# Retention values multiplied token-major, and a fourth tile ahead of the last row of the dilated closing projection

## The chip, the cores and the metric

The kernel runs on one core of a Trainium2 chip. The metric is the device time of one execution in microseconds, as the median of three runs. Everything is computed in fp32: each large product of a weight matrix and activations is made as three matmuls on rounded halves (weight high part times activation high part, high times low, low times high).

## What is computed

Two stacks run over 512 tokens of width 1024. The first has two layers that mix three kinds of attention. The second has a layer of retention with a convolutional feed-forward behind it, then a layer of dilated attention with the same. The change is in the second stack. Cut to what matters:

```python
def retention_mixer(h, w_in, w_out, gn_gain, pos):
    proj = h @ w_in                      # q, k, v and gate; 4 heads, v is 512 wide per head
    ...
    y = retention_chunkwise(q, k, v, log_gamma)
    mu = jnp.mean(y, axis=-1, keepdims=True)
    var = jnp.mean(jnp.square(y - mu), axis=-1, keepdims=True)
    yn = ((y - mu) * lax.rsqrt(var + GN_EPS)).reshape(B, S, dv) * gn_gain
    return (jax.nn.silu(g) * yn) @ w_out

def dilated_mixer(h, w_q, w_o, k_sh, v_sh, pos):
    ...                                  # three groups of windows, 16 heads
    return o @ w_o                       # the closing projection
```

Since the output y is a linear combination of values, taking each value's own mean over its 512 entries away makes the mean of y zero. The kernel does that, before it multiplies with the decayed scores. The input h is a normalised x: the gain goes into the operands, and the factor 1/rms of a token is applied to the product.

## The kernel before

**Layout.** Activations lie channel-major: 128 channels on the partitions, 512 tokens along the free axis, eight tiles k = 0 to 7 (`KT`). The operand of a projection is the pair `HH` and `HL` (high and low part). One output tile of 128 channels is a PSUM bank of 128x512. It takes eight steps of `kt` (L689), and each step is three matmuls with a 128x128 block of weights as the stationary and 512 tokens as the moving operand (L696 to L698).

**Weights.** They come as one stream of blocks in the order in which PE uses them, eight blocks to a chunk, in a ring of three slots. SP loads a chunk, ACT rounds it to `w_hi` (L1196, one for each chunk, once PE is through with the chunk three back), POOL subtracts to get `w_lo` in two halves (L554, L556). The order of the stream is laid out on the host (L2420 to L2442); `beside` interleaves tiles that are multiplied together, k by k.

**Order.** Each engine has its own hand-written program for each stage; they meet by semaphores alone. PE counts steps in `kt_done`, DVE counts emptied banks in `evicted`.

**Retention (PE L952, ACT L1455, DVE L2132), for each of four heads.**
- Four value tiles, channel-major, in banks 0 to 3. DVE multiplies each with the row `RSTD` of 1/rms into `RVF2` (L2146). PE turns it with four 128x128 transposes into bank 6 (`turn`, L953, L961), and ACT copies that into the token-major `RVT` (`v_out`, L1278). In head 0 the first three tiles are multiplied side by side (`together`); the sum of squares, the spread of 1/rms over a bank and the first turn stand behind the fourth.
- Once all four tiles are turned, ACT takes the sum over each token's 512 values (L1481), and DVE adds the negated mean to `RVT` (`centre`, L2152). `centre` stands in DVE's program behind the rotation of both queries and keys (L2157 to L2169).
- Two query and two key tiles in banks 0 to 3, a gate tile in bank 0 and half of another in bank 1. Then the scores of four key blocks (L1004) in banks 4 and 5 by turns, each multiplied with the decay by DVE (L2206), the other half of the gate tile, the product of scores and values (L1018) in banks 6 and 7, and two more gate tiles in banks 2 and 3.
- The previous head's four outputs are finished on DVE between the next head's value tiles (`finish`, L2185 on: two multiplies, a rounding, a subtraction).

**Dilated attention.** Eight pairs of heads (`pair`). While a pair's attention runs, PE multiplies the projections of the next pair. In the last pair there are none, and PE does steps of the closing projection instead: rows k = 0 to 6 of its first three output tiles, 21 steps, in four groups (`out_steps`). Row k needs pair k's output `DO` rounded by ACT (`out_hi`, L1535) and its low part from DVE (`out_lo`, L2288). Rows 0 and 1 are made at the start of the last pair. Row 7 is the last pair's own output: DVE L2319, ACT L1375, DVE L2038. Behind it `linear` does the last row of the three tiles (L900 to L906), then five whole tiles.

```python
t.up("operand")
pe.wait_ge(sems["operand"], t.at("operand"))
for bank in range(3):
    self.kt(bank, hi, lo, KT - 1, False, True)
```

Of the kernel before, what the change touches and what calls it, by code (L numbers as in the profile page):

```python
# [125 lines left out]
for _n, _k in (("mix0", MIX_K), ("ple0", PLE_K), ("mix1", MIX_K), ("ple1", PLE_K), ("ret", RET_K + RETOUT_K),  # L126
# [30 lines left out]
    "decayed", "small", "y_copied", "v_mean", "centred", "ret_squared", "sq_added",  # L157
# [146 lines left out]
def two_stacks_kernel(nc, d, out):  # L304
# [3 lines left out]
    with ExitStack() as ctx:  # L308
# [90 lines left out]
        RVF2 = at("ret_vf", [P, SEQ], 44 * T1)  # L399
# [27 lines left out]
        INV = RC1  # L427

# [148 lines left out]
        def dilated(e):  # L577
            e.dilated()
            e.linear(3, KT, "dil", 1)
# [39 lines left out]
        RS0, RTURN = 4, 6  # L619
        ROTATION = 7  # L620
# [19 lines left out]
        def _(pe):  # L640
            t = Tally(pe)

            class Programs:
# [45 lines left out]
                def kt(self, bank, hi, lo, k, start, stop):  # L689

                    slot, w = self.n // SLOT % RING, slice(self.n % SLOT * P, (self.n % SLOT + 1) * P)
                    if self.n % SLOT == 0:
                        pe.wait_ge(sems["lo_half"], self.n // SLOT + 1)
                    elif self.n % SLOT == SLOT // 2:
                        pe.wait_ge(sems["lo_done"], self.n // SLOT + 1)
                    pe.matmul(banks[bank][:], WH[slot][:, w], hi[:, k, :], start=start, stop=False)  # L696
# [255 lines left out]
                def retention(self):  # L952
                    def turn(tile):  # L953

                        pe.wait_ge(sems["evicted"], tile + 1)
                        if t.k.get("v_token", 0):
                            pe.wait_ge(sems["v_token"], t.at("v_token"))
                        if t.k.get("ret_squared", 0):
                            pe.wait_ge(sems["ret_squared"], t.at("ret_squared"))
                        for b in range(QT):  # L960
                            ins = pe.transpose(banks[RTURN][:, b * P:(b + 1) * P], RVF2[:, b * P:(b + 1) * P], ID[:])  # L961
                        ins.then_inc(sems["v_turned"], t.one("v_turned"))
                        t.up("v_token")
# [6 lines left out]
                    for h in range(RET_HEADS):  # L970
                        v = self.tiles
                        if h == 0:
                            self.together([self.open(b) for b in range(3)], HH, HL, KT, KT)
                            self.open(3)
                            half(3, 0)
                            self.all_squares(OUTB, SQ2)
# [1504 lines left out]
```

## Time and profile before

| | |
|---|---|
| median of three runs | 3018.32 us (3017.38 to 3022.89) |
| profiled execution, its own time | 3016.4 us |
| its span in the trace | 3014.6 us |
| granted TensorE clock, mean | 0.99 of full speed |
| PE busy | 2953.8 us, 98% of the span |
| DVE, ACT, POOL busy | 1734.2, 1055.7, 1282.0 us |
| retention, heads (stretch of the trace) | 1263.8 to 1593.9 us |
| dilated attention, last pair | 2563.7 to 2592.1 us |

"Idle before" in brackets behind a row is the time that the engine stood still before it, and what ended that. Matmul ends are modelled, so the distance from start to start is the one to read. The span lies inside the execution's own time; 1.8 us lie around it.

### The profile page before, as it was taken

Reading aid. Unit: us, or ns where it says so; the run is one execution under the profiler, and the core shown is the slowest. Engines: PE = TensorE matmul, PEld = TensorE weight load, DVE = VectorE, ACT = ScalarE, POOL = GpSimd, SP = SyncE. Lnnn points to the kernel's source line nnn. Section 1 sums busy time; section 2 is a strip of 40 time slices with the busy share of each in tenths; the row PEclk is TensorE's granted clock in tenths of the full one; section 3 lists DMA queues with packets and bytes.
Section 4 is the critical chain, followed back from the end, with each engine's and each line's share of the span. In section 5 each row is a group of like instructions: output and inputs, shape, how many; then the busy total and the mean of one; then the engine's idle time right before and its main releaser. Section 6 shows DMA issues by size and latency. Waiting matters only on the chain.

```text
span 3014.6 us, 39189 instructions
## 1 busy us (share of the span) xinstructions
PE 2953.8 (98%) x15272; PEld 2357.2 (78%) x15272; DVE 1734.2 (58%) x3007; ACT 1055.7 (35%) x1875; POOL 1282.0 (43%) x926
## 2 busy tenths in 40 slices
PE   8999999999999999999999999998999999899998
PEld 6777778877777778877778788886888888688886
DVE  4765455475654555745553587615766666487722
ACT  4444342344443432533332322224333333432221
POOL 3333334453333345534444455544444434355543
PEclk9999999999999999999999999999999999999999
DMA  5222223232222223322222233332222222223332
GB/s 195 78 82 66 70 78 98 84 108 67 84 64 70 78 92 98 103 79 77 77 84 84 77 98 98 98 98 88 78 78 78 78 76 79 64 84 98 98 98 70
DMA packets 78332, 260.22 MB, mean 86 GB/s; under 512 B 10731, under 2 KB 13547, under 8 KB 78149
## 3 DMA queue, kind: packets, MB, share of 16 engines
q1 hardware_dynamic: 77572, 255.63, 27.3%
q8 instruction: 122, 2.00, 0.3%
q10 hardware_dynamic: 576, 2.10, 0.2%
q14 instruction: 62, 0.50, 0.1%
HBM read 255.53 MB, written 6.09 MB: 87 GB/s over the span
## 4 chain that ended last, share of the span: by engine, by line
PE 93%; DVE 4%; ACT 1%; DMA 1%; issue 1%; POOL 0%; SPq 0%; PEldq 0%; DVEq 0%; ACTq 0%; PEld 0%
PE bank L696 27%; PE bank L698 27%; PE bank L697 26%; PE bank L811 2%; PE bank L858 2%; PE bank L838 1%; PE bank L1018 1%; DVE x_res L1788 1%; PE bank L727 1%; PE bank L1054 1%; PE bank L817 1%; DMA bias_copies<-bias_vectors 1%; PE bank L1092 1%; PE bank L1075 1%; DMA w_raw<-in_w 0%
## 5 line engine op out<-in xcount | busy, mean ns | idle before, releaser
L554 POOL TENSOR_TENSOR w_lo<-w_raw,w_hi 128x512 fp32r<-128x512 f32 x458 | 611.3, 1335 | 1649.2 <-ACT w_hi L1196 1649.2
L696 PE MATMUL bank<-h_hi,w_hi 128*128 128x512 f32 x2656 | 1064.9, 401 | 17.9 <-DVE h_lo L1776 6.7
L698 PE MATMUL bank<-h_hi,w_lo 128*128 128x512 f32 x2656 | 1040.2, 392 | 0.0
L697 PE MATMUL bank<-h_lo,w_hi 128*128 128x512 f32 x2656 | 1038.7, 391 | 0.0
L1196 ACT CAST w_hi<-w_raw 128x1024 fp32r<-128x1024 f32 x458 | 480.0, 1050 | 1267.5 <-PE bank L698 1248.0
L556 POOL TENSOR_TENSOR w_lo<-w_raw,w_hi 128x512 fp32r<-128x512 f32 x458 | 667.7, 1458 | 35.9
L696 PEld LDWEIGHTS bank<-h_hi,w_hi 128*128 128x128 f32 x2656 | 501.9, 189 | 129.5 <-issue 22.8
L698 PEld LDWEIGHTS bank<-h_hi,w_lo 128*128 128x128 f32 x2656 | 501.0, 189 | 108.4
L697 PEld LDWEIGHTS bank<-h_lo,w_hi 128*128 128x128 f32 x2656 | 502.5, 189 | 98.3 <-issue 0.6
L2057 DVE TENSOR_SCALAR m<-bank,gains 128x512 f32<-128x512 f32 x48 | 36.1, 751 | 334.5 <-ACT ta L1392 200.3
L1327 ACT ACTIVATE probs<-probs,small_columns 128x128 f32<-128x128 f32 (+2 forms) x192 | 102.0, 531 | 167.2 <-DVE small_columns L1835 163.0
L698 PE MATMUL bank<-f_hi,w_lo 128*128 128x512 f32 x352 | 136.9, 389 | 0.0
L696 PE MATMUL bank<-f_hi,w_hi 128*128 128x512 f32 x352 | 136.9, 389 | 0.0
L697 PE MATMUL bank<-f_lo,w_hi 128*128 128x512 f32 x352 | 136.9, 389 | 0.0
L1830 DVE CUSTOM_DVE_ANT_0 probs<-bank,bias 128x256 f32<-128x256 f32 (+3 forms) x128 | 56.5, 441 | 92.1 <-PE bank L811 88.5
L696 PE MATMUL bank<-zo_hi,w_hi 128*128 128x512 f32 x192 | 77.3, 403 | 0.0
L1337 ACT COPY pt<-bank 128x256 f32<-128x256 f32 (+3 forms) x160 | 55.5, 387 | 62.1 <-PE bank L838 62.0
L696 PEld LDWEIGHTS bank<-f_hi,w_hi 128*128 128x128 f32 x352 | 66.1, 188 | 13.8
L697 PEld LDWEIGHTS bank<-f_lo,w_hi 128*128 128x128 f32 x352 | 66.1, 188 | 13.8
L698 PEld LDWEIGHTS bank<-f_hi,w_lo 128*128 128x128 f32 x352 | 66.1, 188 | 13.5
L698 PE MATMUL bank<-zo_hi,w_lo 128*128 128x512 f32 x192 | 75.0, 391 | 0.0
L697 PE MATMUL bank<-zo_lo,w_hi 128*128 128x512 f32 x192 | 74.8, 390 | 0.0
(288 smaller groups left out, 3950.6 us busy)
## 6 DMA issues: line engine op xcount, KB each, us to landing
w_raw<-in_w SPq DMA_DIRECT2D x458, 512.0 KB, 3.5
bias_copies<-bias_vectors SPq DMA_DIRECT2D x1, 2560.0 KB
x_res<-in_x_t ACTq DMA_DIRECT2D x4, 512.0 KB, 8.2
bias<-bias_copies SPq DMA_DIRECT2D x8, 256.0 KB, 3.3
bias<-bias_copies SPq DMA_DIRECT2D x16, 128.0 KB, 2.4
out_x<-x_res SPq DMA_DIRECT2D x8, 256.0 KB, 2.0
bias_copies<-bias_vectors SPq DMA_DIRECT2D x1, 1280.0 KB
ple_raw<-in_p_t SPq DMA_DIRECT2D x2, 512.0 KB, 3.6
```

Source lines behind the costliest of these rows:

```text
L554: pool.tensor_tensor(WL[slot][:, 0:half], RAW[slot][:, 0:half], WH[slot][:, 0:half].bitcast(F32), ALU.subtract).then_inc(sems["lo_half"], 1)
L556: pool.tensor_tensor(WL[slot][:, half:], RAW[slot][:, half:], WH[slot][:, half:].bitcast(F32), ALU.subtract).then_inc(sems["lo_done"], 1)
L696: pe.matmul(banks[bank][:], WH[slot][:, w], hi[:, k, :], start=start, stop=False)
L697: pe.matmul(banks[bank][:], WH[slot][:, w], lo[:, k, :], start=False, stop=False)
L698: pe.matmul(banks[bank][:], WL[slot][:, w], hi[:, k, :], start=False, stop=stop).then_inc(sems["kt_done"], 1)
L811: ins = pe.matmul(banks[S0 + m][:, 0:blocks * P], AQ[r, q], keys[r, kk], start=True, stop=(kind != "mla"))
L858: ins = pe.matmul(banks[OUTB][r, i * P:(i + 1) * P], v, p[:, b * P:(b + 1) * P], start=(b == 0), stop=(b == blocks - 1))
L1196: act.copy(WH[slot][:], RAW[slot][:]).then_inc(sems["hi_done"], t.one("hi_done"))
L1327: act.activation(s, s, ACT.Exp, bias=sm(NM + u), accum_out=sm(DEN + u)).then_inc(sems["exped"], t.one("exped"))
L1337: act.copy(p[:, 0:w], banks[TURN + m][:, 0:w]).then_inc(sems["pt_copied"], t.one("pt_copied"))
L1830: dve.tensor_tensor_reduce(SS[i % 2][m][:, 0:w], banks[S0 + m][:, 0:w], bias, 1.0, LOWEST, ALU.add, ALU.max, sm(MX + u)).then_inc(sems["dv ...
L2057: dve.tensor_scalar(m[:, tile, :], bank[:], gain(f"{g}{l}", tile), None, ALU.mult).then_inc(sems[step], t.one(step))
```

## The change

1. **Retention values.** The four value tiles of a head become four blocks of 128 tokens with all 512 value channels each. The activations are the stationary operand and 512 columns of weights the moving one. The four blocks take turns at every k, in banks 6, 7, 2 and 3, with three matmuls each. The number of matmuls and their sizes stay: 4 x 8 x 3 of 128x512. `RVF2`, `turn` and its transposes go, and so do the ACT copies of them.
2. **Scaling and centring.** 1/rms is now a factor for each partition; the four columns are kept in `small_columns` (one small DVE copy, once). ACT reads each bank once, scales it and sums it (`accum_out`); DVE negates and divides the sum, and writes the scaled and centred block from the bank to `RVT`. `centre` stands ahead of both rotations.
3. **Order in retention.** In head 0 the sum of squares stands behind k = 4 and the spread behind k = 7, in bank 4. In the other heads the spread stands behind k = 1 and all four `finish` ahead of `centre`.
4. **Closing projection of the dilated layer.** PE does k = 0 to 6 of a fourth tile ahead of the wait for row 7, and then row 7 of all four. Four whole tiles follow.
5. **First operands.** Rows 0 and 1 are made by ACT and DVE at the end of the last but one pair, once its third query tile is through. In the last pair ACT waits for each row by itself.

The weights' order on the host follows. The core of the diff:

```diff
@@ PE
+                        self.rot = 3
+                        fourth = self.rotate()
+                        for k in range(KT - 1):
+                            self.kt(fourth, hi, lo, k, k == 0, False)
                         t.up("operand")
                         pe.wait_ge(sems["operand"], t.at("operand"))
-                        for bank in range(3):
+                        for bank in (0, 1, 2, fourth):
                             self.kt(bank, hi, lo, KT - 1, False, True)
-                        self.rot = 3
...
-                    def turn(tile):
...
+                    def values(k):
+
+                        slot, w = self.n // SLOT % RING, slice(self.n % SLOT * P, (self.n % SLOT + 4) * P)
+                        self.weights_in()
                         for b in range(QT):
...
+                            if k == 0:
+                                self.open(RVALUES[b])
+                            q, out = slice(b * P, (b + 1) * P), banks[RVALUES[b]]
+                            pe.matmul(out[:], HH[:, k, q], WH[slot][:, w], start=(k == 0), stop=False)
+                            pe.matmul(out[:], HL[:, k, q], WH[slot][:, w], start=False, stop=False)
+                            pe.matmul(out[:], HH[:, k, q], WL[slot][:, w], start=False, stop=(k == KT - 1)).then_inc(sems["kt_done"], 1)
+                        self.n += 4
...
+                        for k in range(KT):
+                            if h == 0:
+                                pe.wait_ge(sems["operand"], t.at("operand", k + 1 - KT))
+                            values(k)
+                            if (h, k) == (0, 4):
+                                self.all_squares(RS0, SQ2)
+                            elif (h, k) == (0, KT - 1):
+                                self.spread(RS0)
+                            elif h and k == 1:
+                                self.spread(RS0)
+                        for j in range(4):
                             self.whole(self.open(j))
...
-                        t.up("centred", QT)
-                        pe.wait_ge(sems["centred"], t.at("centred"))
-                        pe.wait_ge(sems["v_token"], t.at("v_token"))
+                        pe.wait_ge(sems["evicted"], v + QT)
@@ ACT
+                        self.past(4, KT)
+                        if h == 0:
+                            t.up("columns_kept")
+                            act.wait_ge(sems["columns_kept"], t.at("columns_kept"))
+                        for b in range(QT):
+                            act.wait_ge(sems["kt_done"], self.n - QT + b + 1)
+                            act.activation(RVT[:, b, :], banks[RVALUES[b]][:], ACT.Copy, scale=sm(XINV + b),
+                                           accum_out=sm(MX + b)).then_inc(sems["v_mean"], t.one("v_mean"))
+                        self.past(4, KT)
...
                         for k in range(2 * i, min(2 * i + 2, KT - 1)):
+                            act.wait_ge(sems["o_used"], self.o + k + 1)
                             act.copy(H2H[:, k, :], DO[:, k, :]).then_inc(sems["operand_hi"], t.one("operand_hi"))
...
+                        if before_last:
+                            act.wait_ge(sems["kt_done"], n + 7 * KT)
+                            out_hi(0)
@@ DVE
+                    row(RS0)
+                    dve.tensor_copy(sm(XINV, QT), sm(INV, QT)).then_inc(sems["columns_kept"], t.one("columns_kept"))
...
                     def centre():
...
+                        self.n += 4 * KT
+                        for b in range(QT):
                             t.up("v_mean")
                             dve.wait_ge(sems["v_mean"], t.at("v_mean"))
-                            dve.tensor_scalar(RVT[:, kt, :], RVT[:, kt, :], sm(MX + kt), None, ALU.add).then_inc(sems["centred"], t.one("centred"))
+                            dve.tensor_scalar(sm(NM + b), sm(MX + b), -1.0 / RET_V, None, ALU.mult).then_inc(sems["dve_step"], t.one("dve_step"))
+                            dve.wait_ge(sems["dve_step"], t.at("dve_step"))
+                            self.tiles += 1
+                            dve.tensor_scalar(RVT[:, b, :], banks[RVALUES[b]][:], sm(XINV + b), sm(NM + b), ALU.mult, ALU.add).then_inc(sems["evicted"], 1)
...
+                        centre()
                         rotary(RQ, 0)
                         rotary(RK, 2)
-                        centre()
...
                             u2(0)
+                            if z == KT - 2:
+                                out_lo(0)
                         else:
-                            out_lo(0)
```

## Rows read from the trace of the kernel before

**Rows 1.** The page: span, busy time of the engines, chain that ended last.

```profile
span 3014.6 us, 39189 instructions
...
PE 2953.8 (98%) x15272; PEld 2357.2 (78%) x15272; DVE 1734.2 (58%) x3007; ACT 1055.7 (35%) x1875; POOL 1282.0 (43%) x926
...
PE 93%; DVE 4%; ACT 1%; DMA 1%; issue 1%; POOL 0%; SPq 0%; PEldq 0%; DVEq 0%; ACTq 0%; PEld 0%
```

**Rows 2.** Waits of PE, whole span: who waited for whom, total us, times, longest.

```profile
PE bank L696 <- DVE h_lo L2038: 3.2, 1, 3.2
PE bank L696 <- DVE h_lo L2288: 1.9, 1, 1.9
```

**Rows 3.** Timeline of PE, head 0: start us, duration, instruction, shapes, count.

```profile
1270.06 0.39 PE L696 MATMUL bank<-h_hi,w_hi 128*128 128x512 f32 x1
...
1275.50 0.39 PE L696 MATMUL bank<-h_hi,w_hi 128*128 128x512 f32 x1
...
1294.74 0.60 PE L961 MATMUL bank<-ident,ret_vf 128*128 128x128 f32 x4
...
1300.67 0.60 PE L961 MATMUL bank<-ident,ret_vf 128*128 128x128 f32 x4
```

**Rows 4.** Windows, heads 0 and 1: length, busy by engine, clock, DMA share, GB/s.

```profile
1263.80:1347.75 83.95, 82.21 (x364) 65.11 (x365) 36.98 (x47) 29.06 (x43) 33.29 (x24) 1.00 0.29 95
1347.75:1429.80 82.05, 81.83 (x365) 65.02 (x364) 44.18 (x53) 26.87 (x39) 33.92 (x24) 1.00 0.26 77
```

**Rows 5.** Timeline, head 0: last sum of squares, first turn.

```profile
1271.98 0.69 DVE L2071 TENSOR_TENSOR sq<-sq 128x512 f32<-128x512 f32 x1
...
1288.76 0.66 PE L961 MATMUL bank<-ident,ret_vf 128*128 128x128 f32 x4 [1.51 <-DVE ret_vf L2146]
```

**Rows 6.** Timeline of DVE, head 1: first and last instruction of one `finish`.

```profile
1354.95 0.74 DVE L2185 SCALAR_TENSOR_TENSOR tc<-ret_y,gains,bank 128x512 f32<-128x512 f32 x1
...
1358.83 0.69 DVE L1621 TENSOR_TENSOR ret_lo<-tc,ret_hi 128x512 fp32r<-128x512 f32 x1
```

**Rows 7.** Timeline, head 0: end of the rotation, centring, scores.

```profile
1314.22 1.67 DVE L2161 TENSOR_TENSOR tc<-tb,ret_sin 128x512 f32<-128x512 f32 x1
...
1319.81 3.59 DVE L2152 TENSOR_SCALAR ret_vt<-ret_vt,small_columns 128x512 f32<-128x512 f32 x4
...
1320.66 3.17 PE L1004 MATMUL bank<-ret_q,ret_k 128*128 128x512 f32 x8
1324.06 1.57 PE L1004 MATMUL bank<-ret_q,ret_k 128*128 128x256 f32 x8 [0.22 <-DVE ret_p L2206]
```

**Rows 8.** Timeline, start of the last dilated pair: ACT, DVE and PE.

```profile
2563.28 0.19 ACT L1516 ACTIVATION_READ_ACCUMULATOR dil_p<-dil_p,small_columns 128x1 f32 x1
2566.67 2.18 ACT L1535 CAST h_hi<-dil_out 128x512 fp32r<-128x512 f32 x4
...
2564.79 0.32 DVE L2281 TENSOR_SCALAR dil_p<-dil_p,small_columns 128x192 f32<-128x192 f32 x1
2565.03 1.08 DVE L2319 TENSOR_SCALAR dil_out<-bank 128x512 f32<-128x512 f32 x1
2567.32 1.29 DVE L2288 TENSOR_TENSOR h_lo<-dil_out,h_hi 128x512 fp32r<-128x512 f32 x2 [1.21 <-ACT h_hi L1535]
...
2568.07 0.50 PE L696 MATMUL bank<-h_hi,w_hi 128*128 128x512 f32 x1 [1.88 <-DVE h_lo L2288]
```

**Rows 9.** Timeline and windows, end of that pair: PE, POOL, granted clock (third last).

```profile
2590.15 1.92 PE L1099 MATMUL bank<-dil_pc,dil_vt 128*64 128x128 f32 x32
2595.30 0.79 PE L696 MATMUL bank<-h_hi,w_hi 128*128 128x512 f32 x1 [3.23 <-DVE h_lo L2038]
...
2590.85 1.27 POOL L556 TENSOR_TENSOR w_lo<-w_raw,w_hi 128x512 fp32r<-128x512 f32 x1
...
2568.00:2572.00 4.00, 3.93 (x17) 3.28 (x18) 3.82 (x14) 3.45 (x11) 0.00 (x0) 1.00 0.00 0
2595.30:2598.00 2.70, 2.70 (x6) 2.14 (x7) 0.48 (x1) 0.00 (x0) 0.00 (x0) 0.50 0.62 194
```

More of the change, by code:

```diff
@@ L687, in rotate, with weights_in @@
                     return self.open((self.rot - 1) % of)
-                def kt(self, bank, hi, lo, k, start, stop):
-                    slot, w = self.n // SLOT % RING, slice(self.n % SLOT * P, (self.n % SLOT + 1) * P)
+                def weights_in(self):
                     if self.n % SLOT == 0:
@@ L695, in kt @@
                         pe.wait_ge(sems["lo_done"], self.n // SLOT + 1)
+                def kt(self, bank, hi, lo, k, start, stop):
+                    slot, w = self.n // SLOT % RING, slice(self.n % SLOT * P, (self.n % SLOT + 1) * P)
+                    self.weights_in()
                     pe.matmul(banks[bank][:], WH[slot][:, w], hi[:, k, :], start=start, stop=False)
@@ L971, in retention @@
                         v = self.tiles
[L972 to L976, printed above, removed]
-                            half(3, KT // 2)
-                            self.spread(OUTB)
-                            turn(v)
-                        else:
-                            for j in range(4):
-                                self.whole(self.open(j))
-                                if j == 0:
-                                    self.spread(RS0)
-                                else:
-                                    turn(v + j - 1)
-                        self.whole(self.open(0))
-                        turn(v + (1 if h == 0 else 3))
-                        for j in range(1, 4):
+                        for k in range(KT):
[9 more added lines that the diff above has]
+                        for j in range(4):
                             self.whole(self.open(j))
-                            if h == 0 and j < 3:
-                                turn(v + j + 1)
                         self.whole(self.open(0))
@@ L2047, in linear @@
                         if tile == 0:
[L2048 removed]
+                            self.n += KT - 1 + 4 if name == "dil" else first * nk
                         elif tile >= first:
@@ L2191, in retention @@
                     for h in range(RET_HEADS):
-                        for j in range(4):
-                            value(h, j)
-                            if h:
+                        if h:
+                            for j in range(4):
                                 finish(h - 1, j)
@@ L2421, in lay_out @@
     for h in range(RET_HEADS):
-        v = plain(ri, 2 * D + RET_V * h, 4)
-        stream += beside(*v[0:3]) + v[3:] if h == 0 else v
+        stream += beside(*plain(ri, 2 * D + RET_V * h, 4))
         stream += plain(ri, 256 * h, 2) + plain(ri, D + 256 * h, 2) + plain(ri, 4 * D + RET_V * h, 4)
@@ L2441, in lay_out @@
     wo = plain(a["att_w_o_2"][0])
-    stream += beside(*wo[0:3]) + wo[3:]
+    stream += beside(*(x[:, :KT - 1] for x in wo[0:3])) + [wo[3][:, :KT - 1]] + beside(*(x[:, KT - 1:] for x in wo[0:4])) + wo[4:]
     stream += up_and_down(1)
```

67 lines of the change are left out of this document (11 added, 56 removed).

## The prediction

> **What bounds the kernel now.** I read the page first. PE is busy 98% of the span, and the chain that ended last lies on it for 93% [rows 1]. So only three things can shorten this kernel: work of PE that goes away, stops of PE that go away, and slow clock. The waits of PE come next. Among them are two single stops at the lines that the change touches in the dilated layer, 3.2 and 1.9 us [rows 2]. Then I went through PE's timeline by stage for its distances from start to start. Two plain matmuls of 128x512 that are 24 apart start 5.44 us apart, 0.227 us each, and that in the stretch of head 0 where three banks take turns [rows 3]. Two turns of value tiles with the same 24 matmuls between them are 5.93 us apart [rows 3]. Whole heads take 83.95 us for the first and 82.05 for the others (heads 2 and 3 repeat head 1 within 0.1), at granted clock 1.00 [rows 4]. DVE and ACT have room (58% and 35% [rows 1]), so what moves between them costs nothing unless PE waits for it.
>
> **Part 1, the values on PE.** The 96 big matmuls of a head stay 96 of the same shape. I take the same 0.227 us for them, since stationary and moving operand only change places and both sides are 128 and 512 wide as before. The four transposes of a turn go: 5.93 - 5.44 = 0.49 us a turn, with what they cost the matmul behind them. Four tiles in four heads make 16 turns: **7.8 us**. The first turn of head 0 also waited 1.51 us for DVE, which had to spread 1/rms and scale a tile first [rows 5]. Behind the new spread stands a query tile that waits for nothing: **1.5 us**.
>
> **Part 2, scaling and centring.** In each head the third block of scores waited 0.22 us for DVE, whose first multiply with the decay stood behind 3.59 us of centring [rows 7]. With the centring ahead of the rotations DVE is free when the first scores arrive. Four heads make 0.9 us; between nothing (the multiply itself becomes the limit) and 0.9 I take **0.9**, as the whole 3.59 us moves away.
> The new centring is hidden, and this is its cover. ACT reads each block in about 0.55 us (a quarter of 2.18) and 0.19 for the sum; DVE needs at most 0.90 us (a quarter of 3.59) and 0.32 for a small step, 4.9 us for four blocks [rows 7, 8]. In heads 1 to 3 it queues behind four `finish`, each 4.57 us (1354.95 to 1359.52) [rows 6], 18.3 together. They start when 1/rms is spread, some 6.4 us into the values (8 steps of three matmuls, and about 1 us, an estimate, for column sums and spread), and end 24.7 us in; the values end near 22.8. So the centring ends near 29.6. The first reader is the third tile behind the values, which reopens bank 2 at 22.8 + 10.9 = 33.7. The cover is 4.1 us; it would be gone at 5.6 us a `finish`. If it is, each further microsecond is a microsecond of PE in three heads.
> Head 0: the last sum of squares ends at 1272.67 [rows 5], and PE wants it after five k of twelve matmuls, 13.6 us behind 1263.8, at 1277.4. No wait. Gate tiles and value blocks at the seam of two heads: block 3 needs the bank of the last gate tile, but nine matmuls (2.0 us) stand between, against one multiply of DVE, 0.69 in the rows nearest to it [rows 5]. Nothing.
>
> **Part 3, the fourth tile ahead of row 7.** Here PE stood 3.23 us, while DVE, ACT and DVE again made row 7 [rows 9]. Now it has 21 matmuls to do, 4.8 us that were due later anyhow. The stop goes: **3.2 us**. Behind the stop the clock was granted at 0.50, the 1.2 GHz level, and six matmuls took 2.70 us in place of 1.36. Behind the stop of 1.88 us the clock stayed at 1.00 [rows 9]. Without the long stop I expect no drop: **1.3 us**, between nothing and 1.3. The weights for it: the steps from the fourth on need the chunk whose first half is ready at 2590.85 [rows 9], while PE is there only at 2592.1 + 2.0. That four tiles and not three end at once gives ACT and DVE one more to empty, beside a next tile of 5.44 us that needs none of their banks. Nothing.
>
> **Part 4, rows 0 and 1 a pair sooner.** PE stood until 2568.07 for the low part of row 0 [rows 8]. ACT is free from 2563.47 and then rounds two rows in 1.1 us, by 2564.6; DVE ends the probabilities at 2565.11 and then makes row 0 by 2565.8. PE was there at 2568.07 - 1.88 = 2566.19. What is late next: DVE's output of pair 6 moves from 2565.03 to 2566.4, and its next scores start near 2567.5 in place of 2568.5, sooner, as the two subtractions no longer stand behind a wait for ACT. PE has 18 matmuls (4.1 us) ahead of the first thing that rests on them. I take **1.8 us**, between 1.0 (the lead of DVE's scores) and 1.9. In ACT's queue the added waits are for things long past (the third query tile, outputs 0 and 1), so nothing is held behind them.
>
> **Sum.** 7.8 + 1.5 + 0.9 + 3.2 + 1.3 + 1.8 = 16.5 us, against the profiled execution's own 3016.4 (span 3014.6 and 1.8 around it): 2999.9. The median of the runs lies 1.9 above that execution, so the forecast for the median is 3018.3 - 16.5 = **3001.8 us**.
>
> **Rivals.**
> *The token-major values lose the clock (slower).* Place: the value stretch, 96 matmuls a head that move to another bank after every three. If that brings small stops and the clock falls to 1.2 GHz, each costs 2.70/6 - 0.227 = 0.22 us more. All 384 cost 86 us, 3087 in all; it cancels the gain from 74 of them, a fifth. Against it: three banks already take turns in head 0, and there the distance is 0.227 us at clock 1.00 [rows 3, 4]. Chance 0.02.
> The Trainium skill (TensorE: Matmul & The Clock Gate, A second HAM failure mode: psum-queue depth-cycling) tells of just such a kernel, in which cycling through PSUM banks made PE idle briefly and its clock swing. By that rule this rival would come true; the rows of head 0 speak against it, since they cycle and stay fast.
>
> *The rotation comes late.* Keys were rotated by 1319.81, 0.85 us ahead of the scores at 1320.66 [rows 7]. Of the six multiplies behind the last key tile two took 1.67 us in place of 0.69. If the order of POOL's work beside them shifts and one more is slow, PE waits 0.1 us a head; if all four others are, 3.9 - 0.85 = 3.1, or 12 us in four heads: 3002 to 3014. Against it: POOL follows the stream of weights, which keeps its place against the key tiles. Chance 0.06.
> The Trainium skill (SBUF — State Buffer, Who interferes with whom) says that a DVE operation with two inputs in SBUF and a GpSimd operation that reads SBUF block one another for a whole instruction. The trace agrees: the 1.67 us row has two SBUF inputs.
>
> *The dilated part pays half.* The clock falls all the same behind the small products, or another wait takes the place of the two removed (the copied probabilities for the next products, say). The clock alone gives 3003; if half of the two stops stays too, 3005.5; if none of part 3 and 4 arrives, 3008.1. This is also the case of a change that doesn't do what it says. Against it: after rows 0 to 6 nothing in the fourth tile depends on the last pair. Chance 0.12.
>
> **How the numbers follow.** The forecast has chance 0.80. 3001.8 is its time. The range goes down to 2998.0 (a median 1 us low, as the lowest run of before, and two or three more us where other stops, such as other half-clock stretches, fall better) and up to 3009.0, which takes in the whole third rival and half of the second. A measurement of this kernel can tell about 0.2%, 6 us: faster than 3012.3 holds for the forecast, the dilated rival and most of the rotation's, 0.93; within it 0.05; slower 0.02.
>
> **What would show it.** Head 1 by the window from its first value matmul to the next head's: 82.05 - 2.0 - 0.2 = 79.9 us, head 0 near 80.3. No transposes at `turn`, matmuls in the values 0.227 apart, clock 1.00. The third block of scores without a wait. The stops of 3.2 and 1.9 us gone from PE's waits, and the row with clock 0.50 behind the first gone too. Wrong would be: distances over 0.227 in the values, a wait on `ret_k` or on the centring, a wait on `w_lo` in the fourth tile, or a new stop of PE in the last pair.

## The result, and the profile after

The median went from 3019.4 us to **2998.0 us** (2994.6 to 3000.4). Each kernel ran four times; the three runs given in front for before are among its four. The ratio is 0.9935, with a 95% interval from 0.9923 to 0.9947, so some 19.6 us or 0.65% went. The forecast was 3001.8 us and a clear gain. The measured median lies 3.8 us below it, at the low end of its range (2998.0) to within the rounding of the runs. The new median of before is 1.1 us higher than the one that the forecast started from, which makes the miss in the gain larger, not smaller: the medians lie 21.4 us apart and the ratio gives 19.6, where the sum said 16.5.

The page of the kernel after: span, busy time, and the chain that ended last.

```profile
span 2996.6 us, 38998 instructions
...
PE 2944.0 (98%) x15208; PEld 2350.6 (78%) x15208; DVE 1722.4 (57%) x3008; ACT 1046.8 (35%) x1859; POOL 1280.2 (43%) x926
...
PE 94%; DVE 3%; DMA 1%; ACT 1%; issue 1%; POOL 0%; SPq 0%; DVEq 0%; ACTq 0%
```

Against [rows 1] the span is 18.0 us shorter, and PE was busy 9.8 us less. PE issued 64 matmuls fewer, which are the sixteen turns of four transposes. So about half of the gain is work and slow clock that PE no longer has, and about half is time in which it stood. PE is still the bound.

The waits of PE after, the longest first (total us, times, longest):

```profile
PE bank L666 <- DMA table<-in_rel_bias: 10.2, 1, 10.2
PE bank L702 <- DVE h_lo L1761: 6.6, 2, 3.3
PE bank L742 <- DVE small_columns L1634: 5.6, 5, 1.4
```

Both rows of [rows 2] are gone, and none of these lies in a stage that was changed. (L702 to L704 are the three matmuls that were L696 to L698.)

**Retention.** Windows over heads 0 and 1 of the kernel after, and twelve us from the end of the last dilated pair over the last row (columns as in [rows 4]):

```profile
1266.23:1346.10 79.87, 79.87 (x349) 63.51 (x350) 34.47 (x48) 27.10 (x39) 33.12 (x24) 1.00 0.30 100
1346.10:1425.86 79.76, 79.76 (x350) 63.43 (x349) 41.07 (x53) 24.72 (x35) 33.45 (x24) 1.00 0.25 80
...
2577.00:2583.00 6.00, 6.00 (x50) 5.06 (x46) 2.98 (x3) 1.68 (x2) 5.01 (x5) 1.00 0.38 111
2583.00:2589.00 6.00, 6.00 (x28) 4.95 (x28) 0.87 (x2) 2.03 (x3) 3.05 (x4) 1.00 0.48 155
```

Head 0 lost 4.1 us and head 1 lost 2.3 [rows 4]; heads 2 and 3 take 79.76 and 79.74. The clock is 1.00 throughout, and PE's busy time is the whole window: no stop is left in a head. The value matmuls, which now change bank after every three, start 0.23 us apart, as before:

```profile
1347.23 0.40 PE L971 MATMUL bank<-w_hi,h_lo 128*128 128x512 f32 x1
1347.46 0.40 PE L972 MATMUL bank<-w_lo,h_hi 128*128 128x512 f32 x1
1347.70 0.40 PE L970 MATMUL bank<-w_hi,h_hi 128*128 128x512 f32 x1
1347.93 0.39 PE L971 MATMUL bank<-w_hi,h_lo 128*128 128x512 f32 x1
...
1369.05 0.39 PE L972 MATMUL bank<-w_lo,h_hi 128*128 128x512 f32 x1
```

From the second to the last of the 96 it is 21.82 us. That is 94 steps of 0.227 us and 0.47 us for the spread of 1/rms between them.

Scores of head 0, timeline of PE and DVE after; the rows of before are in [rows 7]:

```profile
1319.45 4.53 PE L1005 MATMUL bank<-ret_q,ret_k 128*128 128x512 f32 x16
1323.74 0.48 PE L702 MATMUL bank<-h_hi,w_hi 128*128 128x512 f32 x1
...
1326.57 2.75 PE L1017 MATMUL bank<-ret_p,ret_vt 128*128 128x512 f32 x9
...
1317.86 0.69 DVE L2148 TENSOR_TENSOR ret_k<-ret_k,tc 128x512 f32<-128x512 f32 x1
...
1321.43 0.69 DVE L2184 TENSOR_TENSOR ret_p<-bank,ret_decay 128x512 f32<-128x512 f32 x1 [2.88 <-PE bank L1005]
```

All sixteen matmuls of scores run in one go. DVE has been idle for 2.88 us when the first block arrives; before, it was in the middle of centring. The rotation of the keys ends at 1318.55, 0.90 us ahead of the scores (0.85 before). From the first score to the first matmul of the gate tile it is 4.29 us, against 4.73 in before (1320.66 to 1325.39). The wait that went had read 0.22 us, and 0.44 us went.

The new scaling and centring, head 1, on DVE and ACT: first and last instruction of the four `finish`, then the first block.

```profile
1353.12 0.75 DVE L2164 SCALAR_TENSOR_TENSOR tc<-ret_y,gains,bank 128x512 f32<-128x512 f32 x1 [3.47 <-PE bank L742]
...
1368.52 0.69 DVE L1606 TENSOR_TENSOR ret_lo<-tc,ret_hi 128x512 fp32r<-128x512 f32 x1
...
1370.48 0.68 ACT L1465 ACTIVATE ret_vt<-bank,small_columns 128x512 f32<-128x512 f32 x1
1371.06 0.19 ACT L1465 ACTIVATION_READ_ACCUMULATOR ret_vt<-bank,small_columns 128x1 f32 x1
...
1371.37 0.15 DVE L2128 TENSOR_SCALAR small_columns<-small_columns 128x1 f32<-128x1 f32 x1 [2.15 <-ACT ret_vt L1465]
1371.56 0.81 DVE L2131 TENSOR_SCALAR ret_vt<-bank,small_columns 128x512 f32<-128x512 f32 x1
```

Four `finish` take 16.1 us (18.3 were forecast). They end 2.15 us ahead of the first block, and so set nothing. The last block is written at 1375.09, 29.0 us into the head (forecast 29.6), and bank 2 is opened again 11 us behind the values, at 1380.15. By the forecast's reckoning that is 5.1 us of cover, where 4.1 were forecast. The block in bank 2 is the third of the four and is written by 1374.18, so the true cover is 6.0 us.

**The dilated part.** The start of the last pair (ACT, DVE), and the end of that pair (PE, DVE), after:

```profile
2552.04 1.12 ACT L1519 CAST h_hi<-dil_out 128x512 fp32r<-128x512 f32 x2
2553.70 1.28 DVE L2266 TENSOR_TENSOR h_lo<-dil_out,h_hi 128x512 fp32r<-128x512 f32 x2
2554.91 1.05 DVE L2298 TENSOR_SCALAR dil_out<-bank 128x512 f32<-128x512 f32 x1
...
2576.72 1.92 PE L1098 MATMUL bank<-dil_pc,dil_vt 128*64 128x128 f32 x32
2578.57 0.50 PE L702 MATMUL bank<-h_hi,w_hi 128*128 128x512 f32 x1
...
2580.49 1.38 DVE L2023 TENSOR_TENSOR h_lo<-dil_out,h_hi 128x512 fp32r<-128x512 f32 x1 [0.69 <-ACT h_hi L1374]
```

Row 0's low part starts 3.2 us behind the last products of pair 6 (2550.53), and PE's first step of the closing projection, at 2554.61, carries no wait; in before it carried 1.88 us [rows 8]. At the end of the pair PE goes from the products to the fourth tile without a stop. Row 7 is ready at 2581.87, while PE has work ahead until 2583.5. Behind it the clock stays at 1.00 (fourth window above), where before showed 0.50 [rows 9].

**Where the 18.0 us of the two traces lie.** I cut both traces at the same instructions:

| stretch | before | after | less |
|---|---|---|---|
| four heads | 330.13 | 319.13 | 11.0 |
| products of pair 6 to products of pair 7 | 28.29 | 26.19 | 2.1 |
| products of pair 7 to the sums behind the projection | 35.87 | 31.27 | 4.6 |
| all the rest, which no edit touches | 2620.3 | 2620.0 | 0.3 |

The last line hides larger differences that cancel: after loses 2.4 us ahead of the first retention head and gains 2.8 between the heads and pair 6. Half of that gain is a stretch of slow clock at the start of the feed-forward, which comes and goes in this form (granted clock of before, then of after at nearly the same instructions; it ends later in before, and the stretch around it, 1684.91 to 1718.65 there and 1676.36 to 1708.74 in after, is 1.4 us longer):

```profile
1691.30:1696.00 4.70, 4.66 (x11) 3.72 (x12) 4.18 (x7) 2.48 (x4) 0.00 (x0) 0.50 0.00 0
```

```profile
1682.30:1687.00 4.70, 4.68 (x13) 3.71 (x14) 4.18 (x7) 2.49 (x4) 0.00 (x0) 0.58 0.02 3
```

Over all profiles of this study, kernels with the same code there took 965.2 to 967.9 us from the end of the heads to the products of pair 6, and 1263.8 to 1269.7 us up to the first head. The total of a single profile is therefore good to some 6 us only. The stage distances repeat to 0.1 us wherever their code is the same (heads 319.1 in seven traces, pair 26.2 in ten, tail 31.27 in eight), and they are what I compare below. Most of the ratios below have intervals that overlap that of the changed kernel.

### The profile page after: what moved, and what is told of

It is laid out like the page before. It is cut to its first block, busy times and chain, and to the rows that moved or that the text cites. A ratio compares the mean times of both kernels' runs of the same rounds, so it can differ in the third digit from the quotient of the medians.

```text
span 2996.6 us, 38998 instructions
## 1 busy us (share of the span) xinstructions
PE 2944.0 (98%) x15208; PEld 2350.6 (78%) x15208; DVE 1722.4 (57%) x3008; ACT 1046.8 (35%) x1859; POOL 1280.2 (43%) x926
## 4 chain that ended last, share of the span: by engine, by line
PE 94%; DVE 3%; DMA 1%; ACT 1%; issue 1%; POOL 0%; SPq 0%; DVEq 0%; ACTq 0%
PE bank L702 26%; PE bank L704 26%; PE bank L703 26%; PE bank L817 2%; PE bank L864 2%; PE bank L844 1%; PE bank L1017 1%; PE bank L970 1%; PE bank L972 1%; PE bank L971 1%; DVE x_res L1773 1%; PE bank L1053 1%; PE bank L733 1%; DMA bias_copies<-bias_vectors 1%; PE bank L1005 1%; PE bank L823 1%
## 5 line engine op out<-in xcount | busy, mean ns | idle before, releaser
L702 PE MATMUL bank<-h_hi,w_hi 128*128 128x512 f32 x2528 | 1012.8, 401 | 11.7 <-DVE h_lo L1761 6.6
L704 PE MATMUL bank<-h_hi,w_lo 128*128 128x512 f32 x2528 | 990.0, 392 | 0.0
L703 PE MATMUL bank<-h_lo,w_hi 128*128 128x512 f32 x2528 | 989.3, 391 | 0.0
L702 PEld LDWEIGHTS bank<-h_hi,w_hi 128*128 128x128 f32 x2528 | 477.8, 189 | 118.0 <-issue 22.3
L704 PEld LDWEIGHTS bank<-h_hi,w_lo 128*128 128x128 f32 x2528 | 477.3, 189 | 103.2
L703 PEld LDWEIGHTS bank<-h_lo,w_hi 128*128 128x128 f32 x2528 | 478.2, 189 | 93.7 <-issue 0.6
L704 PE MATMUL bank<-f_hi,w_lo 128*128 128x512 f32 x352 | 137.0, 389 | 0.0
L702 PE MATMUL bank<-f_hi,w_hi 128*128 128x512 f32 x352 | 136.9, 389 | 0.0
L702 PE MATMUL bank<-zo_hi,w_hi 128*128 128x512 f32 x192 | 77.3, 403 | 0.0
L702 PEld LDWEIGHTS bank<-f_hi,w_hi 128*128 128x128 f32 x352 | 66.1, 188 | 13.8
L704 PEld LDWEIGHTS bank<-f_hi,w_lo 128*128 128x128 f32 x352 | 66.1, 188 | 13.7
L704 PE MATMUL bank<-zo_hi,w_lo 128*128 128x512 f32 x192 | 75.1, 391 | 0.0
```

Of the source, the lines that this page charges most:

```text
L703: pe.matmul(banks[bank][:], WH[slot][:, w], lo[:, k, :], start=False, stop=False)
L704: pe.matmul(banks[bank][:], WL[slot][:, w], hi[:, k, :], start=False, stop=stop).then_inc(sems["kt_done"], 1)
```

## Experiments

In the expectations, Theory A is the account by terms of the prediction, with the sizes that the trace after gave; the rival of each run stands in its own expectation. "Heads" is the time from the first value matmul of head 0 to the sums behind head 3, "pair" the distance from the products of pair 6 to those of pair 7, and "tail" that from there to the sums behind the projection. Before has 330.1, 28.3 and 35.9 us, after 319.1, 26.2 and 31.3.

### The retention part alone, the dilated part alone

The first run takes points 1 to 3 of the change and leaves points 4 and 5 as they were; the second takes points 4 and 5 alone. The edits are the hunks of the diff.

> The kernel before with the retention part of the change alone. Theory A (the gains are local: transposes, one wait, centring off the path): heads of 79.9, 79.8, 79.8, 79.7 us as in the changed kernel, 11.0 us less than before in the four; the last dilated pair as before (stops of 1.9 and 3.2 us, clock 0.50 behind the second). Time 11 us below before, ratio 0.9963 (0.995 to 0.9975). Theory B (a good part of the gain comes from elsewhere, since the two traces also differ by 2.8 us in stretches that were not changed): heads as above but the time only 8 us below or less.

> The kernel before with the dilated part alone (fourth tile and early rows). Theory A: from the last pair's first transposes to the first sums behind the projection 55.6 us in place of 62.3, heads of retention 83.9 and 82.1 as before; time 6.7 us below before, ratio 0.9978 (0.9965 to 0.999). Theory B: the stop of 3.2 us goes but other stretches of half clock take its place, 4 us or less.

Measured: retention alone 3006.66 us, ratio 0.9967 [0.9954, 0.9979]; heads 319.14, pair 28.28, tail 37.14. Dilated alone 3010.41 us, ratio 0.9981 [0.9972, 0.9991]; heads 330.16, pair 26.20, tail 31.27. The product of the two ratios is 0.9948, inside the interval of the whole change. The intervals are too wide to tell Theory A from Theory B in either run (6 to 14 us for the first, 3 to 8 for the second); the stages tell. Each stage takes on its new time exactly where its own edit is in, so the two parts don't touch one another.

In the trace of the first the two stops are there again, and so is the slow clock behind the second (timeline of PE, then windows):

```profile
2585.23 0.80 PE L702 MATMUL bank<-h_hi,w_hi 128*128 128x512 f32 x1 [3.22 <-DVE h_lo L2018]
```

```profile
2585.23:2587.93 2.70, 2.70 (x6) 2.17 (x7) 0.48 (x1) 0.00 (x0) 0.00 (x0) 0.50 0.61 203
2587.93:2590.60 2.67, 2.67 (x8) 2.09 (x7) 0.00 (x0) 1.06 (x2) 0.00 (x0) 0.50 0.00 0
2590.60:2593.30 2.70, 2.70 (x13) 2.22 (x12) 2.08 (x4) 1.57 (x3) 2.56 (x2) 0.94 0.00 0
```

Here the clock stayed at 0.50 for more than 5 us, in before for less than 3 [rows 9]: the same stop, of the same length, cost 1.3 us more in this execution. So the price of a stop that lets the clock fall has a spread of its own.

### Undoing one dilated edit at a time

The first run undoes point 5 whole: rows 0 and 1 are made where they were before, and ACT waits again for all seven outputs at once and not row by row. The second takes the work of the fourth tile away from ahead of row 7:

```diff
-                        for k in range(KT - 1):
+                        for k in range(0):
                             self.kt(fourth, hi, lo, k, k == 0, False)
...
-                        for bank in (0, 1, 2, fourth):
+                        for bank in range(3):
                             self.kt(bank, hi, lo, KT - 1, False, True)
+                        for k in range(0, KT):
+                            self.kt(fourth, hi, lo, k, k == 0, k == KT - 1)
...
```

> The changed kernel with rows 0 and 1 made at the start of the last pair, as before. Theory A: the stop of 1.9 us is back, last pair up to the last products 26.4 us in place of 24.35, the stretch behind it as in the changed kernel; 2.1 us above the changed kernel. Rival: ACT's own waits row by row in the last pair were what helped, then less than 1 us comes back.

> The changed kernel with the fourth tile wholly behind row 7 (no step of it ahead). Theory A: the stop of 3.2 us is back, and the clock is granted at 0.50 for six or seven matmuls behind it; from the last products to the sums 35.9 us in place of 31.3: 4.6 us above the changed kernel. Rival (the drop of the clock is chance and not due to the stop): the stop alone, 3.2 us.

Measured: late operands 3002.2 us, ratio 0.9953 [0.9939, 0.9967]; pair 28.28, with the stop of 1.88 us back, tail 31.27. Nothing ahead 3003.69 us, ratio 0.9954 [0.9939, 0.9969]; pair 26.22, tail 36.19, with a stop of 3.32 us and, from 0.9 us behind it, slow clock. So point 5 is worth 2.1 us, all of it in the pair, and the fourth tile 4.9 us, all of it in the tail. Neither needs the other.

The rival of the first run, that ACT's waits row by row were what helped, is not tested, as the run undoes them too. The trace of before gives it some weight. There ACT stood for 2.71 us ahead of the two roundings, until DVE had written pair 6's output at 2566.11, which rows 0 and 1 don't need:

```profile
2566.19 0.59 ACT L1278 COPY dil_vt<-bank 128x512 f32<-128x512 f32 x1 [2.71 <-DVE dil_out L2319]
```

How much the waits alone would have brought, without the rows being made a pair sooner, stays open.

### How much has to stand ahead of row 7

The same edit with three steps of the fourth tile, and with one, in place of seven.

> The changed kernel with three steps of the fourth tile ahead of row 7 in place of seven (2.0 us of work under a stop of 3.2). Theory A: a stop of 1.2 us stays, the clock stays at 1.00 behind it, and the stretch from the last products to the sums takes 32.4 to 32.5 us (31.3 with seven steps, 35.9 to 37.1 with none): three steps bring more than their own 2.0 us, since they save the clock too. Rival (the clock falls by what PE did before, not by this stop): 33.7 us or more.

> The changed kernel with one step of the fourth tile ahead of row 7 (0.7 us of work). A stop of 2.3 to 2.6 us stays. Theory A (the clock falls behind long stops only; 1.9 us was short enough, 3.2 too long): nothing seen so far says on which side 2.5 us lies; without a fall 33.8 us from the last products to the sums, with one 35.2 to 36.5. Rival (the fourth tile helps in proportion to its steps): 34.6 us, a seventh of the gain of seven steps.

Three steps: 2999.57 us, ratio 0.9946 [0.9927, 0.9964]; tail 32.53, stop 0.98 us. One step: 3000.23 us, ratio 0.9944 [0.9924, 0.9965]; tail 33.87. In the trace of the latter:

```profile
2581.66 0.50 PE L702 MATMUL bank<-h_hi,w_hi 128*128 128x512 f32 x1 [2.34 <-DVE h_lo L2026]
```

```profile
2581.66:2584.40 2.74, 2.74 (x12) 2.28 (x13) 0.48 (x1) 0.98 (x2) 0.00 (x0) 1.00 0.56 191
```

At this place the clock stays at 1.00 behind a stop of 2.34 us, as it does behind 0.98. Behind 3.22, 3.23 and 3.32 us it fell. So one step, 0.7 us of work, took some 1 us off the stop and the slow clock with it: 2.3 us of tail against none ahead. The other six are worth 2.6 together, which is what was left of the stop.

There is one trace of each of these runs, and other places show that the length of a stop doesn't settle it alone. Early in the run with the retention part alone a stop of 2.32 us was followed by half clock within a microsecond (first two lines), while one of 2.55 us in the run with nothing ahead was not (clock 1.00 from 46.56 to 49.30). In before the clock fell behind the closing projection of the dilated layer, where stops of 0.90 and 1.38 us stand close together (last three lines). So that 2.34 us keeps the clock is what this one trace shows, not a limit.

```profile
50.52 0.30 PE L844 MATMUL bank<-ident,probs 128*128 128x128 f32 x1 [2.32 <-DVE probs L1837]
50.52:53.22 2.70, 2.70 (x9) 2.19 (x10) 2.50 (x11) 2.25 (x6) 0.04 (x1) 0.66 0.48 184
...
2627.87 1.05 PE L727 MATMUL bank<-ones,tb 128*128 128x1 f32 x8 [0.90 <-ACT tb L1392]
2630.30 1.09 PE L736 MATMUL bank<-ident,small_columns 128*128 128x128 f32 x4 [1.38 <-DVE small_columns L1649]
2630.30:2634.73 4.43, 1.09 (x4) 0.71 (x5) 3.01 (x5) 1.24 (x2) 0.00 (x0) 0.50 0.40 120
```

### What the transposes cost

Four transposes of a 128x128 tile into bank 5, which is free here, behind every second k of the values, on top of the changed kernel. Nothing reads them.

```diff
                             values(k)
+                            if k % 2:
+                                if 5 in self.last:
+                                    pe.wait_ge(sems[self.last[5][0]], self.last[5][1])
+                                for b in range(QT):
+                                    pe.transpose(banks[5][:, b * P:(b + 1) * P], ID[:], ID[:])
```

> The changed kernel with four transposes of the identity put behind every second k of the values (16 groups in four heads, nobody waits for them). Theory A: they cost what a turn took beyond its matmuls, 0.47 us a group, so heads of 81.7 us in place of 79.8 and 7.6 us in all. Rival (the turns were dear for their waits and copies on other engines, not for PE's own work): less than 4 us.

Measured: 3004.27 us, ratio 0.9962 [0.9951, 0.9973] (the changed kernel has 0.9935). Heads 326.52 us, 7.39 more for 16 groups: 0.46 us a group, clock 1.00:

```profile
1346.20:1427.80 81.60, 81.60 (x366) 65.04 (x365) 39.60 (x53) 24.72 (x36) 33.79 (x25) 1.00 0.25 78
```

This is the first term by itself. It is the group in PE's queue that costs, and not what surrounded it.

### A new bank at every matmul

The four blocks take turns after each single matmul, not after three: four of high times high, four of low times high, four of high times low.

```diff
-                        for b in range(QT):
...
-                            pe.matmul(out[:], HH[:, k, q], WH[slot][:, w], start=(k == 0), stop=False)
-                            pe.matmul(out[:], HL[:, k, q], WH[slot][:, w], start=False, stop=False)
...
+                        for part in range(3):
+                            for b in range(QT):
+                                if part == 0:
                                    pe.matmul(out[:], HH[:, k, q], WH[slot][:, w], start=(k == 0), stop=False)
...
```

> The changed kernel with the four banks of the values changing after every matmul in place of every third. Theory A (changing banks is free): heads of 79.8 us, clock 1.00, time as the changed kernel within 2 us. Rival (cycling through banks brings small stops and a lower clock): value matmuls more than 0.227 us apart; if the clock falls, up to 0.22 us more for each of 384.

Measured: 2997.73 us, ratio 0.994 [0.992, 0.9961], and head 1:

```profile
1345.83:1425.74 79.91, 79.82 (x349) 63.50 (x348) 41.08 (x53) 24.74 (x35) 33.42 (x24) 1.00 0.26 79
```

Heads 1 to 3 take 79.91, 79.93 and 79.95 us. Three times as many changes of bank cost 0.20 us a head at most, and the clock stays at 1.00. The rival that the values lose the clock by taking turns is ruled out by more than the change itself needed.

### The centring one place later

`centre` stands between the rotation of the queries and that of the keys, with the banks handed over to match:

```diff
+                        rotary(RQ, 0)
                         centre()
-                        rotary(RQ, 0)
                         rotary(RK, 2)
...
```

> The changed kernel with the centring between the rotations of queries and keys. Theory A (its place ahead of both is what hides it, since the first key tile needs bank 2 back): PE stops some 10 us at the first key tile of every head, until DVE has ended the query rotation (7 us) and three blocks (2.7 us), and starts again at half clock for some microseconds: heads of 90 to 93 us, 40 to 52 us in all. Rival (the centring is hidden wherever it stands, as DVE is busy half the time): under 5 us.

Measured: 3047.59 us, ratio 1.0107 [1.0086, 1.0128]. Heads 367.60 us, 48.5 more than after. The waits of PE, and the windows behind the first of the four stops:

```profile
PE bank L702 <- DVE ret_vt L2135: 39.8, 4, 9.9
```

```profile
1308.27:1311.00 2.73, 2.73 (x7) 2.15 (x8) 0.81 (x2) 0.00 (x0) 0.00 (x0) 0.50 0.00 0
1311.00:1315.00 4.00, 4.00 (x18) 3.29 (x17) 0.00 (x0) 0.00 (x0) 0.00 (x0) 0.92 0.02 4
```

In each head PE waits 9.9 us for the bank of a centred block, and the slow clock behind it costs most of the other 2. So the one reader that the prediction gave for the cover, the tile that opens bank 2 again, is the right one. The place of `centre` ahead of both rotations is not a matter of taste: it is the difference between a gain of 2.3 us in each of heads 1 to 3 and a loss of nearly 10.

### DVE kept busy ahead of the decay

The centring stays where the change put it, and four plain multiplies of the same shape, into scratch tiles that nothing reads, stand where it was before.

```diff
                         rotary(RK, 2)
+                        for b in range(QT):
+                            dve.tensor_scalar((TA, TB, TC, VAR)[b][:], RVT[:, b, :], 1.0, None, ALU.mult).then_inc(sems["dve_step"], t.one("dve_step"))
+                            dve.wait_ge(sems["dve_step"], t.at("dve_step"))
```

> The changed kernel with four DVE operations of the old centring's kind (128x512 from SBUF to SBUF, unused results) behind the rotation, where the centring stood before. Theory A (of the 82.05 - 79.76 = 2.29 us of a head 0.4 come from there, more than the 0.22 that the trace shows as idle, since the matmuls behind the stop start slower too): from the scores to the next products 7.5 to 7.6 us in place of 7.12, heads of 80.2 us. Rival (only the idle 0.22 counts): 7.3 us, heads of 80.0.

Measured: 3001.42 us, ratio 0.995 [0.9934, 0.9965]. Heads 321.88 us, 0.69 a head more. Timeline of head 0, PE and DVE:

```profile
1319.09 3.17 PE L1005 MATMUL bank<-ret_q,ret_k 128*128 128x512 f32 x8
1322.74 1.57 PE L1005 MATMUL bank<-ret_q,ret_k 128*128 128x256 f32 x8 [0.48 <-DVE ret_p L2187]
1324.07 0.47 PE L702 MATMUL bank<-h_hi,w_hi 128*128 128x512 f32 x1
...
1318.23 1.40 DVE L2181 TENSOR_SCALAR ta<-ret_vt 128x512 f32<-128x512 f32 x1
...
1321.99 1.16 DVE L2187 TENSOR_TENSOR ret_p<-bank,ret_decay 128x512 f32<-128x512 f32 x2
```

The filler was a little longer than the old centring (1318.23 to 1321.99, 3.76 us, against 3.59), so the stop became 0.48 us and not 0.22. From the scores to the gate tile it is 4.98 us, 0.69 more than after. Both numbers of the expectation were too low (a head of 80.2 us, where 80.44 was measured), and the rival's are further off. The stop comes back with the work ahead of the decay, which settles its cause. And it costs 0.21 us more than its idle time, as the old one did (0.44 for 0.22).

### The spread of the retention projection one step later

A last one for a gain. Behind the heads the closing projection of retention spreads its 1/rms at k = 1, and PE stands 0.46 us there, in before as in after. At k = 2 it should find the sums ready.

```diff
-                        if k == 1 and spread is not None:
+                        if k == 2 and spread is not None:
```

> The changed kernel with the spread of 1/rms in the projection behind retention one k later (behind six steps in place of three). Theory: the stop of 0.46 us there goes, and DVE, which then starts the last four outputs 2 us later, is not awaited, as twelve k of three steps stand ahead of the first operand that it makes. 0.5 us less in that stage and nothing in the time that can be told. Rival: the last operands come late and PE stops at the 13th k, up to 1.5 us.

The row in after, then in the experiment:

```profile
1588.98 0.65 PE L742 MATMUL bank<-ident,small_columns 128*128 128x128 f32 x4 [0.46 <-DVE small_columns L1634]
```

```profile
1591.44 0.60 PE L742 MATMUL bank<-ident,small_columns 128*128 128x128 f32 x4
```

The stop is gone and no other takes its place; from the end of the heads to the next sums it is 88.46 us against 89.15, 0.69 us less where 0.5 was expected. The whole takes 2998.84 us, ratio 0.9937 [0.9921, 0.9954]. That 0.69 us cannot be told from the changed kernel by its time; the stage shows it, the median doesn't. No version beats the changed kernel measurably.

## Why the prediction was right, and where its terms were off

| term | forecast | in the traces | by itself |
|---|---|---|---|
| sixteen turns | 7.8 | 7.4 | 7.4 (transposes back) |
| first turn's wait | 1.5 | 1.8 | |
| scores behind centring | 0.9 | 1.8 | 2.8 with a longer stop |
| stop of 3.2 us and slow clock | 4.5 | 4.6 | 4.9 |
| rows 0 and 1 | 1.8 | 2.1 | 2.1 |
| sum | 16.5 | 17.7 | |

**What bounds it.** Right. PE was taken as the bound, every gain as work or a stop of PE, and 17.7 of the 18.0 us between the traces lie in the three stretches that the prediction named. The sum was 1.2 us too low, and two terms, the scores (1.8 us) and the early rows (2.1 us), came out above the upper bounds that the prediction gave them (0.9 and 1.9). That the measured median stood on the low edge of the range, and not below it, is luck: two of the four runs lie under 2998.0. The prediction had read the profile by stage and not by shares. DVE's load is a percentage point lower and would have told nothing.

**The turns.** Right to 0.4 us. A head's 2.29 us, less 0.44 for the scores, leaves 1.85 for four turns, 0.46 each. The forecast read 0.49 from one distance [rows 3].

**The scores: the term that was mis-sized.** The step "the third block of scores waited 0.22 us ... four heads make 0.9 us" took the idle time as the price. The distance from start to start shows twice that, 4.73 against 4.29 us. The profile of before had the row for it, and the prediction itself says that distances are what to read; for this term it read the bracket.

**The same in the others.** Put the idle time of each stop beside what its stage lost, in the runs where the clock stayed at 1.00:

| stop | idle, us | stage longer by, us |
|---|---|---|
| scores, before | 0.22 | 0.44 |
| spread behind retention, in after | 0.46 | 0.69 |
| scores, DVE kept busy | 0.48 | 0.69 |
| row 7, three steps ahead | 0.98 | 1.26 |
| rows 0 and 1 late | 1.88 | 2.08 |
| row 7, one step ahead | 2.34 | 2.60 |

Each costs 0.2 to 0.3 us more than it reads. The first turn's wait fits: head 0 lost 4.07 us, less 2.29 like the others is 1.78, for an idle time of 1.51. Against the forecast this makes 0.9 us more in the scores, 0.3 in the first turn and 0.3 in the early rows. With 0.1 in the tail, and less the 0.4 by which the turns were set too high, these are the 1.2 us between the two sums. That the extra is time in which PE gets going again is my reading; which matmuls it falls on isn't shown, as their ends are modelled.

**The stop ahead of row 7 and the slow clock.** Right in size (4.6 for 4.5) and in mechanism: the clock doesn't fall when the stop is gone. The slow stretch has a spread of its own, though. The same stop cost 4.6 in before, 4.9 and 5.9 us in two runs that had it back. "Between nothing and 1.3" for the clock was too narrow at the top: one execution paid 2.4.

**The early rows.** Right in size to 0.3 us. Whether the gain comes from making them sooner, as the prediction has it, or in part from ACT's waits row by row, isn't shown. What was named as late next, DVE's output of pair 6 and the next scores, was late by nothing that PE noticed.

**The cover of the centring.** Right to 0.6 us: it ends 29.0 us into the head against 29.6. The `finish` were shorter than the one that was read. [rows 6] is one of the slow kind, and 4 x 4.57 us took all four for slow, an error on the safe side. That the tile which reopens bank 2 is the first reader is shown by the run with the centring one place later.

**The rivals.** The clock lost to changing banks: there is no sign of it, even at a change with each matmul. The paragraph of the Trainium skill that the prediction weighed against this (TensorE: Matmul & The Clock Gate, A second HAM failure mode: psum-queue depth-cycling) tells, for a bf16 kernel, of gaps in PE's work that go with the cycling. Here the cycling came without gaps, and the clock held. The rotation late: it ended 0.90 us ahead of the scores. The dilated part at half: every part of it arrived. The chances don't quite add up: the forecast (0.80), the dilated rival (0.12) and most of the rotation's (0.06) make 0.95 or more for a clear gain, not 0.93.

**The rest of the difference in the medians.** The terms make 17.7 us of the 18.0 between two single executions. The medians differ by 21.4, and their ratio allows for 16 to 23. The other 3.4 us are where the two profiled executions lie among their own runs, which spread over 5.5 and 5.9 us: that of before is 3.0 us below its median (3016.4 against 3019.4), that of after 0.4 above. Up to the first retention head, where no edit is, the trace of before has the shortest time of all thirteen traces (1263.8 us, the others 1264.0 to 1269.7). And beside the experiments the kernel before had medians of 3015.2, 3017.6 and 3018.2 us over 13, 11 and 8 runs, all below 3019.4. So nothing asks for a term that the prediction left out; why executions differ in the stretches that no edit touches isn't shown.

## What to carry to other kernels

When PE is the bound, read a stop of it from start to start over the instructions around it, and not from the idle time in its bracket: here every stop cost 0.2 to 0.3 us more. So many short stops are worth more than they look. Of a stop so long that the clock falls behind it, the first microsecond taken off may be worth two; in the one trace taken here one step of work that was due anyway brought 2.3 us, and the next six 2.6. And where work on another engine moves, write down the one instruction that next needs its bank and how long it has until then: one place later cost 12 us a head.

## What the runs showed of the hardware that was not expected

- A stop of PE cost 0.20 to 0.28 us beyond its idle time, at the six lengths from 0.22 to 2.34 us that were seen (the table above).
- In the changed stages the granted clock stayed at 1.00 behind stops of 0.98, 1.88 and 2.34 us and went to 0.50, the 1.2 GHz level, behind 3.22 to 3.32 and 9.9 us. Elsewhere it also fell behind 2.32 us (in the run with the retention part alone) and behind 0.90 and 1.38 us close together (in before), and held behind 2.55 us (in the run with nothing ahead). How long it stayed there varied between executions at the same place and the same stop: six matmuls in before, fourteen in the run of the retention part alone.
- A multiply with a constant of a 128x512 tile on DVE took 0.43 us, or 1.37 to 1.40 beside POOL's subtractions (1317.76 to 1320.75 in the run with DVE kept busy): three times as long. The roundings in `finish` do the same, 0.43 or 1.40 us. So a stretch of DVE has a length that depends on where POOL's work falls: four `finish` took 4.7, 3.7, 2.9 and 4.7 us. The Trainium skill (SBUF — State Buffer, Who interferes with whom) says that copies, casts and such multiplies of DVE can use the port pair that it shares with GpSimd, and that one of the two then waits out the other's whole instruction; these rows agree with it.
